# Two elementwise steps of a chunked SSD scan exchanged between VectorE and GpSimd

## The reference

```python
def step(h, inp):
    xc, dtc, Bc, Cc = inp
    acs = jnp.cumsum(dtc * Ar, axis=1)
    seg = acs[:, :, None] - acs[:, None, :]
    decay = jnp.exp(jnp.where(tril, seg, -jnp.inf))
    xdt = xc * dtc[..., None]
    cb = jnp.einsum('blgn,bsgn->blsg', Cc, Bc)
    y_diag = jnp.einsum('blsg,blsgr,bsgrp->blgrp', cb, decay, xdt)
    y_off = jnp.einsum('blgn,bgrpn,blgr->blgrp', Cc, h, jnp.exp(acs))
    to_end = jnp.exp(acs[:, -1:] - acs)
    h_new = jnp.exp(acs[:, -1])[..., None, None] * h + jnp.einsum('bsgn,bsgr,bsgrp->bgrpn', Bc, to_end, xdt)
    return h_new, y_diag + y_off
```

## Time and profile before

| | before |
|---|---|
| median of 3 runs | 4136.58 us (4136.21 to 4139.23) |
| the profiled execution, its own time | 4137.26 us |
| its span in the profile | 4135.5 us |
| mean granted TensorE clock | 0.946 |
| busy over the span: PE / PEld / DVE / ACT / POOL | 3731.1 / 2912.8 / 1979.2 / 921.7 / 358.0 us |

### The profile page before, as it was taken

How to read it: one execution, slowest core, us unless ns; L and a number is a source line. 1 busy time by engine, 2 the same in 40 slices (tenths; PEclk the granted TensorE clock), 3 DMA queues, 4 the chain that set the end, 5 groups by cost and what they waited for, 6 DMA issues and landing times. The chain is left out here.

```text
span 4135.5 us, 47625 instructions
## 1 busy us (share of the span) xinstructions
PE 3731.1 (90%) x17940; PEld 2912.8 (70%) x17940; DVE 1979.2 (48%) x4316; ACT 921.7 (22%) x1992; POOL 358.0 (9%) x372
## 2 busy tenths in 40 slices
PE   5999999996996999999677499699998799999996
PEld 3888888884654888888555366455565588888885
DVE  3444444441123889674399632244520344444444
ACT  2111111112131222222387200256100211111111
POOL 0000000000000000000065211454000000000000
PEclk8999999998998999999887699899989899999998
DMA  4333333215431222322367332100222122222221
GB/s 185 123 123 123 113 124 124 109 61 202 122 99 67 72 82 82 101 84 79 116 218 224 92 110 79 52 16 6 82 62 77 46 83 91 83 91 82 91 82 72
DMA packets 172232, 406.36 MB, mean 98 GB/s; under 512 B 25880, under 2 KB 102888, under 8 KB 150488
## 3 DMA queue, kind: packets, MB, share of 16 engines
q1 hardware_dynamic: 158296, 360.48, 25.9%
q10 hardware_dynamic: 10512, 21.78, 1.5%
q0 software_dynamic: 3200, 21.11, 1.4%
HBM read 335.35 MB, written 68.14 MB: 98 GB/s over the span
## 5 line engine op out<-in xcount | busy, mean ns | idle before, releaser
L572 ACT ACTIVATE f_u<-f_Y 128x258 f32<-128x258 f32 x408 | 157.4, 386 | 1099.9 <-PE f_Y L510 1099.9
L653 DVE TENSOR_TENSOR f_g<-f_u,f_Z 128x258 f32<-128x258 f32 x136 | 57.6, 423 | 390.8 <-PE f_Z L510 390.8
L925 PE MATMUL ps_pp<-h,ps_w 128*128 128x344 f32 x720 | 219.0, 461 | 23.6 <-DMA ps_w<-in_w_att 23.6
L925 PEld LDWEIGHTS ps_pp<-h,ps_w 128*128 128x128 f32 x720 | 135.9, 192 | 104.1 <-DMA ps_w<-in_w_att 24.2
L510 PE MATMUL f_Y<-h,raw 128*128 128x258 f32 x704 | 172.7, 389 | 33.9 <-PEq L111 33.9
L623 DVE TENSOR_TENSOR f_g<-f_u,f_X 128x258 f32<-128x258 f32 x136 | 57.6, 423 | 293.1 <-PE f_X L510 292.8
L510 PEld LDWEIGHTS f_Y<-h,raw 128*128 128x128 f32 x704 | 134.2, 193 | 61.9 <-issue 42.9
L510 PE MATMUL f_Y<-f_tc,f_sums 128*128 128x258 f32 x704 | 167.5, 380 | 2.1 <-DVE f_sums L394 2.1
L510 PE MATMUL f_Y<-f_tc,raw 128*128 128x258 f32 x704 | 167.7, 380 | 0.9 <-ACT f_u L572 0.9
L510 PE MATMUL f_Y<-h,f_sums 128*128 128x258 f32 x704 | 167.6, 381 | 1.0 <-ACT f_u L572 1.0
L510 PE MATMUL f_X<-h,raw 128*128 128x258 f32 x704 | 168.3, 382 | 0.0
(11 more groups left out here) (437 smaller groups left out, 7450.3 us busy)
## 6 DMA issues: line engine op xcount, KB each, us to landing
raw<-in_w_f1i SPq DMA_DIRECT2D x44, 1024.0 KB, 4.8
raw<-in_w_f2i SPq DMA_DIRECT2D x44, 1024.0 KB, 4.8
f_wa<-in_w_ada SPq DMA_DIRECT2D x14, 2048.0 KB, 9.7
dn_raw<-in_w_dense SPq DMA_DIRECT2D x28, 1024.0 KB, 5.6
raw<-in_w_f1o SPq DMA_DIRECT2D x16, 1024.0 KB, 4.8
sg_ab<-scr_acs SPq DMA_DIRECT2D x32, 512.0 KB, 5.4
raw<-in_w_f2o SPq DMA_DIRECT2D x16, 1024.0 KB, 4.8
scr_xc<-dn_cv SPq DMA_DIRECT2D x24, 512.0 KB, 4.5
```

The lines of the kernel that those rows point to most:

```text
L572: nc.scalar.activation(u[:, i % 2, n], bank[i % 2][:, 0:SUB], ACT.Copy).then_inc(done, 1)
L653: nc.vector.tensor_tensor(g[:, i % 2, 1], u[:, i % 2, 1], Z[i % 2][:, 0:SUB], ALU.add).then_inc(zread, 1)
L925: m = nc.tensor.matmul(pp[n % 2][:, 0:NC], w[:, t % WR, k], h[:, k, c * NC:(c + 1) * NC], start=k == 0, stop=k == KT - 1)
```

## The change

The two products change places between the engines. POOL now does `fade(i + 1)` where it did `scale(i + 1)`. DVE now does `scale(i + 1)`, and not at the place of the old `fade`, behind `skip(i)`, but ahead of `skip(i)`, right behind `weigh(i + 1)`. Operands, shapes and semaphores of both are as before; only the engine that waits and counts up is another.

```diff
@@ POOL
-            def scale(n):
-                pool.wait_ge(grown, UP + later(n))
-                pool.wait_ge(turned, UP + n + 1)
-                nc.gpsimd.tensor_tensor(Cs[:, n % 2], Cs[:, n % 2], st[:, n % RS, GT + 1].unsqueeze(1).to_broadcast([P, R, P]),
-                                        ALU.mult).then_inc(c_s, 1)
+            def fade(n):
+                pool.wait_ge(hup, UP + n)
+                nc.gpsimd.tensor_tensor(v3(hd[:, n % 2]), v3(hT[:, (n - 1) % 2]), wide(etot, n), ALU.mult).then_inc(h_d, 1)
@@ POOL, the loop
                 if i + 1 < N and (i + 1) % TB:
-                    scale(i + 1)
+                    fade(i + 1)
@@ DVE
-            def fade(n):
-                dve.wait_ge(hup, UP + n)
-                nc.vector.tensor_tensor(v3(hd[:, n % 2]), v3(hT[:, (n - 1) % 2]), wide(etot, n), ALU.mult).then_inc(h_d, 1)
+            def scale(n):
+                dve.wait_ge(grown, UP + later(n))
+                dve.wait_ge(turned, UP + n + 1)
+                nc.vector.tensor_tensor(Cs[:, n % 2], Cs[:, n % 2], st[:, n % RS, GT + 1].unsqueeze(1).to_broadcast([P, R, P]),
+                                        ALU.mult).then_inc(c_s, 1)
@@ DVE, the loop
                 if i + 1 < N:
                     weigh(i + 1)
+                if i + 1 < N and (i + 1) % TB:
+                    scale(i + 1)
                 if i < N:
                     skip(i)
-                if i + 1 < N and (i + 1) % TB:
-                    fade(i + 1)
                 if i < N:
                     gate(i)
```

## The result

The changed kernel takes 4146.99 us in the median of 11 runs (4142.93 to 4151.07), the kernel before 4136.75 in the 11 runs beside it, 10.2 us less. The ratio worked out from all these runs is 1.0027, 95% interval 1.0017 to 1.0036, or 7 to 15 us more. The forecast was +5.7 us, 4142.3. The measured time lies in the range (4118 to 4148) and above the forecast's own (4141 to 4144), and by 0.27% it falls just beyond the 0.2% that the forecast called no change.

A forecast was written before the change was run, and what follows sets the result against it. DVE was taken to set the pace, with POOL's instructions holding it. 26 steps at +0.24 us (+6.2) and the second step's -0.6 gave +5.7 us, 4142.3 us; range 4118 to 4148, the forecast's own 4141 to 4144.

The forecast's parts named there:

- DVE sets the pace, and the two engines hold each other: Phase 2030 to 2330 us: DVE paces; its instructions with both inputs in SBUF and POOL's don't run at once.
- signs: Profile after: POOL's fade about 2.0 us, DVE's scaling about 2.07, E's multiplication 1.46 to 1.48, DVE without idle time.
- The durations of the moved products: Unheld work on the new engines: scaling 1.21 us on DVE, fade 1.04 us on POOL.
- twin: Similar traced instruction lending its duration: E's multiplication (1.21 us) for DVE's scaling, `xw` (1.04 us) for POOL's fade.
- POOL gets in between two multiplications of DVE: POOL's fade runs after E's multiplication and before DVE's scaling, which stands until 2165.26 and ends at 2166.47.
- rival A: DVE runs E's multiplication and the scaling before POOL gets in; -0.61 us per step, 4119.3 us; 17%.
- +0.24 us per step: On DVE the gate starts at 2167.42 where it was 2167.18; over 26 steps +6.2 us.
- a plain step of 8.05 us: Predicted length of a step without a norm instruction in the profile after, where it was 7.81 us.
- The second step's saving of 0.57 us: Its `cbm` is no longer held (1.93 us) and its fade gives 0.61, against +1.97 for the scaling.
- The chunk load costs nothing: SP's load leaves some 2 us later, when the skip term ends; taken at nothing.
- rival B: Later chunk load makes DVE wait ahead of `xdt` or `hT`; if 12 steps were hit, +7 us, 4149; 9%.
- Rival C: Moved products longer than taken: fade 1.26 us gives 4148.2, scaling 1.36 gives 4146.4, both 4152; 9%.

The follow-up runs named there:

- Each half alone: Two runs against the kernel before: only the scaling moved to DVE, 4135.29 us (ratio 0.9994); only the fade moved to POOL, 4148.73 us (1.0024).

## Why the prediction was right in its mechanism and short in its size

- *DVE sets the pace, and the two engines hold each other* (read from the earlier trace rows): right. Fade 2.02 us on POOL and scaling 2.06 on DVE are what the text gave as signs (2.0 and 2.07). Each half alone moved the time as its holds say, one by nothing and one up.
- *The durations of the moved products*: right. The scaling's twin of 1.21 us is its bare duration in three runs, and the fade's twin of 1.04 us is its own where nothing holds it.
- *POOL gets in between two multiplications of DVE* (against rival A): right in all 28 steps. Rival A's 1.21 us scaling does not occur after the change; it does in one step of the run with the gate behind the update, so what was forecast here is not without exception.
- *+0.24 us per step*: too small, and this is the term that failed. From the skip term's start to the next start the forecast took 1.03 us from the earlier trace rows, where the fade followed. Now the gate follows, which needs the skip term's result, and the start comes at 1.15. The 0.12 us belongs to every step that had a fade there: 26 x 0.12 = 3.1 us, and the step grew by 0.36 to 0.39 us. By the forecast's own sign (a plain step of 8.05 us that comes out of the durations) this is a miss: the durations came, and the step is 8.20 us long, since the wait is in none of them. From the `cbm` of the second step (2068.13 before, 2067.40 after) to the last instruction of the phase DVE took 9.5 us longer, where 5.7 had been forecast. Of these, from start to start, the two products make +7.9 (7.6 forecast), the `cbm` of the second step -1.8 (-1.9), the gap behind the skip term +3.1 (nothing), and the gate +0.2. The ends of that stretch, before:

```profile
2339.22 0.22 DVE L2397 TENSOR_TENSOR S<-S,sg_pH 128x64 f32<-128x64 f32 x1
```

and after:

```profile
2067.40 0.29 DVE L2277 TENSOR_TENSOR sg_cbm<-sg_bt,upper 128x128 f32<-128x128 f32 x1 [8.18 <-ACT sg_bt L2177]
...
2347.96 0.22 DVE L2397 TENSOR_TENSOR S<-S,sg_pH 128x64 f32<-128x64 f32 x1
```

The row that showed the gap was in the trace of before, in a step without a fade, where the gate starts 0.04 us behind the skip term's end and not the usual 0.08 ahead of it:

```profile
2181.30 1.11 DVE L2310 SCALAR_TENSOR_TENSOR h<-sg_st,dskip,sg_pY 128x128 f32<-128x128 f32 x4
2182.45 0.69 DVE L2299 TENSOR_TENSOR h<-h,sg_zt 128x512 f32<-128x512 f32 x1
```

- *The second step's saving of 0.57 us*: from `cbm` to the gate it went from 5.51 to 5.08 us, -0.43. Of the 0.14 that is missing, 0.12 is the same wait.
- *The chunk load costs nothing* (rival B): right. TensorE's transposes did wait for it more (13 waits, 19.7 us in all, where it was 7 waits and 11.4 us), landing took 6.7 us at most, and DVE has no wait behind it. *Rival C* falls with the durations.
- *The range*: that 4146.99 lies inside it is partly luck. The range goes above 4144 only to take in the cheaper half of rivals B and C, and neither happened; the 0.12 us that did was in no term and no rival.
- Of the 9.5 us, 8.4 are left in the span: DVE came to the second step 0.7 us sooner in this profile (0.9 sooner already at the `xdt` of 2048.54, ahead of the first changed instruction), and what follows the phase took 0.3 us less, without a line of the change in it. The runs' +7 to +15 us hold both figures.

## What to carry to other kernels

Before an elementwise product is moved between VectorE and GpSimd, lay the two timelines beside each other and mark which VectorE instructions are held by GpSimd's and which are not; the place in the order decided more here (4147 against 4121 us for the same exchange) than which engine did the work. In the two runs that moved the reduction, an instruction that isn't held was cover for one GpSimd instruction only: moved from under one, it left the next held instruction to stand there. And where an instruction is taken out from between a producer and its reader on the same engine, count the reader's wait for the producer, here 0.12 us a step.

## What the runs showed of the hardware that was not expected

The engine that already stood ready nearly always got in ahead of the other's next instruction, although that followed with no gap: POOL's fade went between two multiplications of DVE that started one behind the other in 28 of 28 steps of the changed kernel, and in 27 of 28 with the gate behind the update. Also, instructions with a single tile in SBUF and a per-partition scalar were held too, unlike the skip term: the eight TENSOR_SCALAR on `diag` took 1.66 us at the phase's end, where POOL was idle, and 2.65 in the kernel before with the reduction moved, under `T`:

```profile
2155.68 2.65 DVE L2336 TENSOR_SCALAR sg_diag<-ident,sg_root 128x128 f32<-128x128 f32 x8
```
